# A third expert's second matrix loaded ahead, with the memory map and the load order changed to make room

## The chip, the cores and the metric

One core of a Trainium2 chip runs the whole program. The metric is the device time of one execution in microseconds (us); lower is better. The engines are TensorE (PE in the profile, its weight loads PEld), VectorE (DVE), ScalarE (ACT), GpSimd (POOL) and SyncE (SP); an engine's own queue of transfers and waits is written SPq or ACTq.

## The reference, cut to what matters

Two decoder layers over 512 tokens of width 1024, all in float32. Each layer has a mixer (layer 0: sliding-window attention and RWKV-7; layer 1: gated linear attention), a cross-attention into 256 memory tokens, and a hierarchical mixture of experts (MoE). In the MoE a token picks one group of 8 experts, then its two best experts in it. Of 32 experts each has three matrices of 2 MB:

```
y = (silu(x @ w1[e]) * (x @ w3[e])) @ w2[e]      # w1, w3: 1024 x 512, w2: 512 x 1024
x = x + sum over the token's two experts of gate * y
```

So both layers together read 64 experts of 6 MB, some 400 MB.

## The kernel before

**Places.** SBUF holds XT (the residual, transposed), HT (16 KB a partition), a ring of six 16 KB tiles W0 to W5, and a 72 KB region WORK that is laid out anew for each stage. Within WORK the cross-attention has its scaled input XC at 40 to 56 KB (what the queries are made from) and a head's turned scores xpT at 56 to 60 KB; the MoE has hk (the normalised rows) and later WX at 8 to 24 KB, routing tables from 24 KB, and the expert loop's own tiles (xg, xgT, ysb, hs, sl, act, spread) from 42 KB.

**The expert loop.** Expert blocks have 64 rows and are taken in pairs, i = 0, 1, 2, ...; both layers have 16 pairs here (`trips`). Block b = 0 of a pair uses W3, W4 (w1, w3) and W5 (w2), block b = 1 uses W0, W1 and W2. The order on PE for a pair is: `up(0, i)` (16 products of w1 and w3), `down(1, i-1)` (8 products of w2), turning the hidden rows, `up(1, i)` with the previous pair's results added to XT between its steps (`add_tiles`), turning, `down(0, i)` with the turning of the next pair's rows in its middle. At `k == 4` an `up` counts `hh_half`, at its end `hh_done`; a `down` counts `y_done`.

**Loads.** SP issues the weight loads, all in one queue. A buffer is loaded again as soon as its readers are through: `up(b, i)` on SP waits for `hh_half` and loads the first halves of w1 and w3 (two transfers of 1 MB), then waits for `hh_done` and loads the second halves; `down(b, i)` waits for `y_done` and loads w2 (one transfer of 2 MB). Buffers hold one pair, so a load is issued about a pair before its use.

**What is loaded ahead.** Block 0's expert goes into W3 to W5 long before (`first_expert`). Block 1's three matrices are issued in `experts` when the cross-attention's output product is through (`res_done`), since W0 to W2 hold that stage's weights until then. The third expert (pair 1, block 0) takes its w1 into HT after the rows have been turned (`h_turned`) and its w3 into WX, which lies over hk and so waits until hk has been read and stored to HBM (`rows_made`, `h_stored`; ACT stores the rows into `hrows`, from which POOL gathers each pair's rows by index into xg). Its w2 goes into W5 like any later one, when block 0 of pair 0 is done. The stream of the remaining loads begins when the routing tables are there (`plan_v`): SP then reads the number of trips and each expert's number from SBUF.

```
sp.wait_ge(s["res_done"], 16 * (L + 1))
up_weights(L, 1, slice(1, 2))
down_weights(L, 1, slice(1, 2))
sp.wait_ge(s["h_turned"], TT * (L + 1))
extra_matrix(HT, ...)
sp.wait_ge(s["rows_made"], 4 * L + 2)
sp.wait_ge(s["h_stored"], 16 * TT * (L + 1))
extra_matrix(WX, ...)
sp.wait_ge(s["plan_v"], PLAN_V * (L + 1))
```

**After layer 0's loop** the last `down`, four `add_tiles` on PE with an addition each on DVE, squares on ACT and their sum on POOL lead into layer 1's first projection, whose weights od_q, od_k, od_v0 are loaded into W0, W1, W2.

Of the kernel before, what the change touches and what calls it, by code (L numbers as in the profile page):

```python
# [18 lines left out]
I32 = mybir.dt.int32  # L19
# [4 lines left out]
P = 128  # L24
SEQ, D, MEM = 512, 1024, 256
# [18 lines left out]
BLK = 64  # L44
# [12 lines left out]
SUM_BANKS = ((0, 1), (5, 7))  # L57
MEMORY_AT = ((0, 1, 2), (3, 4, 5), (6, 7))
# [94 lines left out]
def trunk(nc, a, hrows, out):  # L153
    with ExitStack() as ctx:
# [160 lines left out]

        lg, lx = tab("lg", [P, TT, NR]), tab("lx", [P, TT, NX])
# [11 lines left out]
        nit, nitf = tab("nit", [P, 2], I32), tab("nitf", [P, 2])  # L328
        bei, bef = tab("bei", [P, NBLK], I32), tab("bef", [P, NBLK])
        idx = tab("idx", [P, NPAIR], I32)  # L330
        slot_gate, slot_tok = tab("slot_gate", [P, NPAIR]), tab("slot_tok", [P, NPAIR])
        rhot, comb = tab("rhot", [P, 8, HB]), tab("comb", [P, 8, 2, NBLK])
        cmp = tab("cmp", [P, (NBLK - NX) * NX])
        M3 = WORK + 42 * KB
        assert table[0] <= M3
        xg = sb("xg", [P, D], at=M3)
        xgT = sb("xgT", [P, 2, KD, BLK], at=M3 + 4 * KB)
        ysb = sb("ysb", [P, D], at=M3 + 8 * KB)
        hs = [sb(f"hs{b}", [P, FF], at=M3 + 12 * KB + 2 * KB * b) for b in range(2)]
        sl = [sb(f"sl{b}", [P, 4, BLK], at=M3 + 16 * KB + KB * b) for b in range(2)]  # L340
        act_ = [sb(f"act{b}", [P, 4, BLK], at=M3 + 18 * KB + KB * b) for b in range(2)]
        spread = sb("spread", [P, 2 * P], at=M3 + 20 * KB)
        osb = sb("osb", [P, TT, D], at=WORK + 24 * KB)
# [36 lines left out]
        def _(sp):  # L380
# [34 lines left out]

            def up_half(L, b, e, half):
# [9 lines left out]
            def down_weights(L, b, e):  # L426
                sp.dma_start(W4[EXPERT[b] + 2], a["moe_w2"][L][e][0].rearrange("(p k) n -> p k n", p=P)).then_inc(w2_in[b], 16)

            def extra_matrix(dst, matrix):
                sp.dma_start(dst[:, :, :], matrix.rearrange("(p k) n -> p k n", p=P)).then_inc(s["extra_in"], 16)  # L430

            def experts(L, pairs):
# [33 lines left out]
                down(0, 1)  # L466
                down(1, 1)
                up(1, 2)
                down(0, 2)
# [1986 lines left out]
```

## Time and profile before

| | |
|---|---|
| median of 3 runs | 1855.28 us (1853.74 to 1870.42) |
| the profiled execution | 1862.81 us, its span 1861.0 us, mean granted clock 0.99 |
| PE busy | 1754.9 us (94%) |
| DVE, ACT, POOL busy | 539.8, 524.4, 169.5 us (29%, 28%, 9%) |
| chain that ended last | PE 57%, DMA 35% of the span |
| moved by DMA | 466.40 MB; HBM read 468.12 MB |

A busy PE here is one with matmuls in flight. The times in the sections below are of this one profiled execution, in us from its start. Layer 0's expert loop lies at about 514 to 993, layer 1's at about 1370 to 1846.

### The profile page before, as it was taken

What the parts mean: (1) busy time and instruction counts of PE and PEld (TensorE: products, weight loads), DVE (VectorE), ACT (ScalarE), POOL (GpSimd) and SP (SyncE); (2) the same over time, 40 slices, a digit from 0 to 9 for tenths busy, and PEclk for the clock granted to TensorE, in tenths of its full rate; (3) what the DMA queues carried; (4) which work ended last, traced back from release to release, by engine and by line L of the source; (5) the groups of instructions that cost most, each with busy time, mean ns of one, the idle gap of its engine ahead of it and who ended that gap; (6) DMA issues with size and microseconds to landing.
All of it is one profiled execution on the core that took longest, in us unless ns stands there. A gap on an engine that the chain in (4) does not pass through costs nothing.

```text
span 1861.0 us, 23577 instructions
## 1 busy us (share of the span) xinstructions
PE 1754.9 (94%) x9202; PEld 844.7 (45%) x9202; DVE 539.8 (29%) x973; ACT 524.4 (28%) x934; POOL 169.5 (9%) x208
## 2 busy tenths in 40 slices
PE   8999899999999989898999999999999998989898
PEld 4555777455433333333334443686443333333333
DVE  2154555322332313131313004212242231313133
ACT  3244342243422221212123004423332222121213
POOL 2000351020100000000001000221100000000000
PEclk9999799999999999999999999999999999999999
DMA  7210100160399999999994113104099999999995
GB/s 193 91 46 1 47 2 2 68 255 20 130 391 422 423 422 423 424 423 421 418 390 173 47 45 133 48 1 184 0 375 424 423 423 422 423 424 423 423 421 201
DMA packets 88564, 466.40 MB, mean 251 GB/s; under 512 B 22319, under 2 KB 24479, under 8 KB 48058
## 3 DMA queue, kind: packets, MB, share of 16 engines
q1 hardware_dynamic: 77600, 450.98, 59.8%
q0 software_dynamic: 4608, 7.92, 1.2%
q10 hardware_dynamic: 6298, 6.68, 1.1%
q8 instruction: 43, 0.70, 0.2%
q14 instruction: 15, 0.12, 0.0%
HBM read 468.12 MB, written 6.29 MB: 255 GB/s over the span
## 4 chain that ended last, share of the span: by engine, by line
PE 57%; DMA 35%; DVE 4%; ACT 2%; SPq 1%; issue 1%; POOL 0%; ACTq 0%; DVEq 0%; POOLq 0%
PE ps L1092 52%; DMA W<-in_moe_w 33%; PE ps L1301 2%; DMA hrows<-hk 2%; SPq L419 1%; ACT hk L1015 0%; DVE CS L1987 0%; PE ps L1782 0%; PE ps L1819 0%; DVE XI L2120 0%; POOL sqo L600 0%; DMA xin<-in_x 0%; PE ps L1530 0%; PE ps L1238 0%; DVE XJ L2056 0%
## 5 line engine op out<-in xcount | busy, mean ns | idle before, releaser
L1092 PE MATMUL ps<-W,xgT 128*64 128x512 f32 x1984 | 458.2, 599 | 24.4 <-DMA W<-in_moe_w 22.9
L1092 PE MATMUL ps<-HT,W 128*128 128x512 f32 (+2 forms) x896 | 337.4, 533 | 4.3 <-DVE HT L1952 1.4
L1092 PE MATMUL ps<-W,act 128*64 128x512 f32 x1024 | 240.0, 601 | 33.4 <-DMA W<-in_moe_w 33.4
L1092 PEld LDWEIGHTS ps<-W,xgT 128*64 128x64 f32 x1984 | 131.2, 136 | 273.3 <-issue 235.7
L1092 PEld LDWEIGHTS ps<-HT,W 128*128 128x128 f32 (+1 forms) x896 | 166.3, 188 | 163.1 <-issue 151.0
L1048 ACT ACTIVATE ysb<-ps 32x512 f32<-32x512 f32 x248 | 146.0, 589 | 267.2 <-PE ps L1092 265.0
L2381 DVE TENSOR_TENSOR XT<-ps,XT 128x512 f32<-128x512 f32 x248 | 159.6, 685 | 182.8 <-PE ps L1092 182.8
L2375 DVE TENSOR_TENSOR act<-ps,sl 128x256 f32<-128x256 f32 x64 | 26.9, 420 | 473.8 <-ACT sl L1041 473.8
L1037 ACT ACTIVATE hs<-ps 128x512 f32<-128x512 f32 x64 | 38.2, 597 | 441.5 <-PE ps L1092 441.5
L1092 PE MATMUL ps<-spread,ysb 64*128 64x256 f32 x992 | 140.4, 402 | 3.2 <-DVE ysb L2401 1.7
L1092 PEld LDWEIGHTS ps<-W,act 128*64 128x64 f32 x1024 | 65.9, 136 | 160.4 <-issue 107.9
L1092 PEld LDWEIGHTS ps<-spread,ysb 64*128 64x128 f32 x992 | 85.6, 186 | 108.0 <-DVE XT L2381 49.6
L633 POOL COPY idc<-idx 128x1 int32 (+1 forms) x32 | 5.8, 182 | 862.7 <-PE ps L1782 804.7
L1092 PE MATMUL ps<-W,HT 128*128 128x512 f32 (+1 forms) x192 | 63.2, 488 | 0.0
L1092 PE MATMUL ps<-xo,W 128*128 128x512 f32 x128 | 56.3, 595 | 0.0
L1092 PE MATMUL ps<-XC,W 128*128 128x512 f32 x128 | 56.1, 592 | 0.0
L2371 DVE COPY xgT<-ps 128x1024 f32<-128x1024 f32 x32 | 39.2, 1224 | 51.5 <-PE ps L1782 51.5
L1933 DVE TENSOR_TENSOR XT<-ps,XT 128x512 f32<-128x512 f32 (+1 forms) x32 | 20.0, 624 | 115.1 <-PE ps L1092 115.1
L1092 PEld LDWEIGHTS ps<-W,HT 128*128 128x128 f32 x192 | 31.4, 191 | 32.2 <-issue 32.2
L1819 PEld LDWEIGHTS ps<-ident,hs 128*128 128x128 f32 x256 | 26.8, 140 | 40.6 <-issue 24.3
L1819 PE MATMUL ps<-ident,hs 128*128 128x128 f32 x256 | 42.0, 287 | 2.8 <-ACT hs L1037 2.8
L1782 PEld LDWEIGHTS ps<-ident,xg 128*128 128x128 f32 x256 | 27.4, 141 | 27.5 <-issue 24.3
(422 smaller groups left out, 1598.6 us busy)
## 6 DMA issues: line engine op xcount, KB each, us to landing
W<-in_moe_w SPq DMA_DIRECT2D x248, 1024.0 KB, 17.8
W<-in_moe_w SPq DMA_DIRECT2D x64, 2048.0 KB, 23.4
W<-in_od_w_in SPq DMA_DIRECT2D x6, 2048.0 KB, 8.1
W<-in_ev_w_in SPq DMA_DIRECT2D x3, 2048.0 KB, 7.8
W<-in_xa_wq SPq DMA_DIRECT2D x2, 2048.0 KB, 8.5
W<-in_xa_wo SPq DMA_DIRECT2D x2, 2048.0 KB, 11.9
hrows<-hk ACTq DMA_DIRECT2D x8, 512.0 KB, 15.8
HT<-in_moe_w SPq DMA_DIRECT2D x2, 2048.0 KB, 16.9
```

The lines of the kernel that those rows point to most:

```text
L419: sp.dma_start(W8[EXPERT[b]][:, k4, :], w1[:, k4, :]).then_inc((wa_in, w13_in)[half][b], 16)
L633: g.tensor_copy(idc[:, :], column).then_inc(s["gb_step"], 1)
L1037: sc.activation(hs[b][:, :].rearrange("p (k q) -> p k q", k=4), ps[:, 2 + b, :].rearrange("p (q k) -> p k q", k=4), ACT.Copy).then_inc(s[" ...
L1048: ins = sc.activation(ysb[o:o + HB, 512 * h:512 * h + 512], ps[r:r + HB, 6, :], ACT.Copy)
L1092: return te.matmul(o, l, r, start=first, stop=last)
L1301: return te.matmul(o, l, r, start=first, stop=False, skip_group_check=True)
L1782: ins = te.transpose(ps[:, k // 4, P * (k % 4):P * (k % 4) + P], xg[:, k * P:k * P + P], ident[:, :])
L1819: ins = te.transpose(ps[:, 4, f * P:f * P + P], hs[b][:, f * P:f * P + P], ident[:, :])
L1933: ve.tensor_tensor(XT[:, mt, cols], ps[:, at + mt % 2, cols], XT[:, mt, cols], ALU.add).then_inc(s["xt_ready"], 1)
L2371: ve.tensor_copy(by_rows(xgT), ps[:, 0:2, :].rearrange("p w (g b c) -> p (w g) b c", g=8, b=2)).then_inc(s["xgT_in"], 1)
L2375: ve.tensor_tensor(act_[b][:, :, :], ps[:, 4, :].rearrange("p (f c) -> p f c", f=4)[:, :, BLK:2 * BLK], sl[b][:, :, :], ALU.mult).then_inc ...
L2381: return ve.tensor_tensor(x, ps[:, SUM_BANKS[m % 2][h], :].rearrange("p (k t q) -> p k t q", k=2, t=2), x, ALU.add)
```

## The change

- Each layer loads the third expert's w2 ahead as well, into a new tile WY at 44 to 60 KB of WORK, over XC and xpT of head 2 (`extra_second`, after `sm_pv` has counted head 2's product). PE's `down(0, 1)` reads it there. The load of w2 for pair 1, block 0, into W5 is gone; W5 takes pair 2's at that place instead (`down(0, 2, readers=1)`), ahead of `down(1, 1)`.
- Block 1's matrices are issued as each ring tile comes free. Layer 0: w1 and w3 after the memory values (`DONE["xv"]`), then WY, then w2 after the output product. Layer 1: w2 after the mixer's output product, w1 after the queries, WY, and w3 (whole, `up_matrix`) after the cross-attention's output product.
- Every load of a w2 and of a third expert's matrix is made of two transfers of half the size.
- Hidden rows, gates, activations and results (hs, sl, act, ysb) lie from 26 KB of WORK, over routing tables that are no longer read; the tables still read in the loop stand below 26 KB. xg, xgT, spread and osb move.
- At the end of layer 0, od_q and od_k are loaded once the last `up` is through (`hh_done`), od_v0 as before; the four `add_tiles` write four different pairs of PSUM banks, and only the last one waits for a DVE addition, the first.

```
+FINAL_BANKS = ((5, 7), (4, 6), (2, 3), (5, 7))
...
+        OVER = WORK + 26 * KB
...
+        spread = sb("spread", [P, 2 * P], at=WORK + 42 * KB)
+        WY = sb("WY", [P, 4, D], at=WORK + 44 * KB)
+        xg = sb("xg", [P, D], at=WORK + 4 * KB)
+        xgT = sb("xgT", [P, 2, KD, BLK], at=WORK + 60 * KB)
+        hs = [sb(f"hs{b}", [P, FF], at=OVER + 2 * KB * b) for b in range(2)]
...
+            def up_matrix(L, b, e, m):
+                w = a[("moe_w1", "moe_w3")[m]][L][e][0].rearrange("(p k) n -> p k n", p=P)
+                for half, k4 in enumerate((slice(0, 4), slice(4, 8))):
+                    sp.dma_start(W8[EXPERT[b] + m][:, k4, :], w[:, k4, :]).then_inc((wa_in, w13_in)[half][b], 16)
...
             def down_weights(L, b, e):
-                sp.dma_start(W4[EXPERT[b] + 2], a["moe_w2"][L][e][0].rearrange("(p k) n -> p k n", p=P)).then_inc(w2_in[b], 16)
+                w2 = a["moe_w2"][L][e][0].rearrange("(p k) n -> p k n", p=P)
+                for f in (slice(0, 2), slice(2, 4)):
+                    sp.dma_start(W4[EXPERT[b] + 2][:, f, :], w2[:, f, :]).then_inc(w2_in[b], 16)
...
             def extra_matrix(dst, matrix):
-                sp.dma_start(dst[:, :, :], matrix.rearrange("(p k) n -> p k n", p=P)).then_inc(s["extra_in"], 16)
+                n = dst.shape[1]
+                m = matrix.rearrange("(p k) n -> p k n", p=P)
+                for part in (slice(0, n // 2), slice(n // 2, n)):
+                    sp.dma_start(dst[:, part, :], m[:, part, :]).then_inc(s["extra_in"], 16)
+
+            def extra_second(L):
+                sp.wait_ge(s["sm_pv"], 7 + 4 * L)
+                extra_matrix(WY, a["moe_w2"][L][EXTRA:EXTRA + 1][0])
...
-                def down(b, i):
+                def down(b, i, readers=0):
                     e = expert(b, i)
-                    sp.wait_ge(s["y_done"], i * 2 + (pairs * 2 + (b + L + 1)))
+                    sp.wait_ge(s["y_done"], (i - readers) * 2 + (pairs * 2 + (b + L + 1)))
+                    if readers:
+                        sp.sem_inc(w2_in[b], 32)
                     down_weights(L, b, e)
 
-                sp.wait_ge(s["res_done"], 16 * (L + 1))
-                up_weights(L, 1, slice(1, 2))
-                down_weights(L, 1, slice(1, 2))
+                if L == 0:
+                    sp.wait_ge(s["proj_done"], DONE["xv"][1])
+                    up_weights(L, 1, slice(1, 2))
+                    extra_second(L)
+                    sp.wait_ge(s["res_done"], DONE["xo0"][1])
+                    down_weights(L, 1, slice(1, 2))
+                else:
+                    sp.wait_ge(s["res_done"], DONE["od_o1"][1])
+                    down_weights(L, 1, slice(1, 2))
+                    sp.wait_ge(s["proj_done"], DONE["xq1"][1])
+                    up_matrix(L, 1, slice(1, 2), 0)
+                    extra_second(L)
+                    sp.wait_ge(s["res_done"], DONE["xo1"][1])
+                    up_matrix(L, 1, slice(1, 2), 1)
...
                 up(0, 2, readers=1)
                 up(1, 1)
-                down(0, 1)
+                down(0, 2, readers=1)
                 down(1, 1)
                 up(1, 2)
-                down(0, 2)
                 with sp.Fori(3, trips) as i:
...
-            sp.wait_ge(s["y_done"], pairs * 2 + 2)
+            sp.wait_ge(s["hh_done"], pairs * 2 + 2)
             for name, _ in LOADS[LAYER0_LOADS:]:
+                if name == "od_v0":
+                    sp.wait_ge(s["y_done"], pairs * 2 + 2)
                 load(name)
...
-                    if m >= 2:
-                        pe.wait_ge(s["xt_ready"], n["xt"] + 2 * (m - 1))
-                    add_tiles(m)
+                    if m == 3:
+                        pe.wait_ge(s["xt_ready"], n["xt"] + 2)
+                    add_tiles(m, FINAL_BANKS[m])
```

## Rows read from the trace of the kernel before

**Rows 1.** The page: the span in 40 slices of 46.5 us, busy tenths.

```profile
PE   8999899999999989898999999999999998989898
DMA  7210100160399999999994113104099999999995
```

**Rows 2.** The chain of waits that ended last: start, duration (us), work.

```profile
577.02 1.87 PE ps L1092 x8
...
605.09 1.87 PE ps L1092 x8
...
610.59 22.81 DMA W<-in_moe_w
...
695.33 4.89 PE ps L1092 x24
...
726.34 4.89 PE ps L1092 x24
...
972.73 11.80 PE ps L1092 x64
...
1493.56 23.76 DMA W<-in_moe_w
...
1825.67 11.80 PE ps L1092 x64
```

**Rows 3.** Windows: length, busy us by engine, granted clock, DMA share, GB/s.

```profile
500.00:518.00 18.00, 15.20 (x112) 9.02 (x114) 14.91 (x67) 9.34 (x13) 0.00 (x0) 1.00 1.02 427
...
532.00:552.00 20.00, 18.56 (x94) 6.75 (x92) 2.07 (x3) 5.94 (x11) 1.19 (x2) 1.00 1.02 424
552.00:560.00 8.00, 8.00 (x44) 3.08 (x46) 3.86 (x6) 0.23 (x1) 0.00 (x0) 1.00 1.02 430
...
1530.00:1800.00 270.00, 245.62 (x1250) 92.80 (x1248) 63.36 (x103) 59.25 (x107) 10.80 (x18) 1.00 1.01 423
```

**Rows 4.** The timeline of SP's queue, layer 0: issue time, issue duration, line, transfer.

```profile
495.79 0.33 SPq L419 DMA_DIRECT2D W<-in_moe_w  x1
...
505.67 0.33 SPq L430 DMA_DIRECT2D HT<-in_moe_w  x1
524.26 0.33 SPq L430 DMA_DIRECT2D WX<-in_moe_w  x1
526.26 0.37 SPq L419 DMA_DIRECT2D W<-in_moe_w  x1
...
569.75 0.33 SPq L419 DMA_DIRECT2D W<-in_moe_w  x1
```

**Rows 5.** The timeline of SP's queue, layer 1, the same load.

```profile
1424.42 0.34 SPq L419 DMA_DIRECT2D W<-in_moe_w  x1
```

**Rows 6.** The timeline of ACT: its first store of rows.

```profile
502.97 0.35 ACTq L1019 DMA_DIRECT2D hrows<-hk  x1
```

**Rows 7.** The chain of waits: the last store of rows.

```profile
507.58 16.60 DMA hrows<-hk
```

**Rows 8.** The timeline of DVE: the end of the routing tables.

```profile
520.59 0.15 DVE L2359 CAST nit<-nitf 128x1 int32<-128x1 f32 x1
```

**Rows 9.** The timeline of PE, both layers: in brackets, idle before and its releaser.

```profile
535.09 1.09 PE L1782 MATMUL ps<-ident,xg 128*128 128x128 f32 x8 [1.39 <-DMA xg<-hrows,idc]
...
1403.65 1.94 PE L1092 MATMUL ps<-W,xgT 128*64 128x512 f32 x8 [0.45 <-DMA W<-in_moe_w]
```

**Rows 10.** DMA issues of 524.2 to 524.5: KB, us from issue to landing.

```profile
WX<-in_moe_w SPq DMA_DIRECT2D x1, 2048.0 KB, 7.6
```

**Rows 11.** DMA issues of 570.1 to 570.5.

```profile
W<-in_moe_w SPq DMA_DIRECT2D x1, 1024.0 KB, 16.2
```

**Rows 12.** DMA issues of 1424.8 to 1425.

```profile
W<-in_moe_w SPq DMA_DIRECT2D x1, 1024.0 KB, 14.6
```

**Rows 13.** DMA issues of the whole span: a 1 MB load with no other beside it.

```profile
memin<-in_mem ACTq DMA_DIRECT2D x1, 1024.0 KB, 5.0
```

**Rows 14.** The timeline of POOL after layer 0's loop.

```profile
999.36 9.71 POOL L600 TENSOR_TENSOR sqo<-sqo 128x512 f32<-128x512 f32 x7 [38.81 <-ACT sqo L715]
```

More of the change, by code:

```diff
@@ L314, in tab @@
             return sb(name, shape, dt, at=table[0] - -(-size // 32) * 32)
+        nit, nitf = tab("nit", [P, 2], I32), tab("nitf", [P, 2])
+        bei, bef = tab("bei", [P, NBLK], I32), tab("bef", [P, NBLK])
+        idx = tab("idx", [P, NPAIR], I32)
+        slot_gate, slot_tok = tab("slot_gate", [P, NPAIR]), tab("slot_tok", [P, NPAIR])
+        OVER = WORK + 26 * KB
+        assert table[0] <= OVER
         lg, lx = tab("lg", [P, TT, NR]), tab("lx", [P, TT, NX])
@@ L327, in trunk @@
         blk, brk = tab("blk", [P, 8]), tab("brk", [P, 8])
[L328 to L331, printed above, removed]
         rhot, comb = tab("rhot", [P, 8, HB]), tab("comb", [P, 8, 2, NBLK])
         cmp = tab("cmp", [P, (NBLK - NX) * NX])
[L334 to L343, printed above, removed]
+        assert table[0] <= WORK + 42 * KB
+        spread = sb("spread", [P, 2 * P], at=WORK + 42 * KB)
[3 more added lines that the diff above has]
+        hs = [sb(f"hs{b}", [P, FF], at=OVER + 2 * KB * b) for b in range(2)]
+        sl = [sb(f"sl{b}", [P, 4, BLK], at=OVER + 4 * KB + KB * b) for b in range(2)]
+        act_ = [sb(f"act{b}", [P, 4, BLK], at=OVER + 6 * KB + KB * b) for b in range(2)]
+        ysb = sb("ysb", [P, D], at=OVER + 8 * KB)
+        osb = sb("osb", [P, TT, D], at=WORK + 44 * KB)
         fin = sb("fin", [P, D], at=WORK + 64 * KB)
@@ L1783, in turn_rows, with add_tiles @@
                     ins.then_inc(s["xg_turned"], 1)
-                def add_tiles(m):
+                def add_tiles(m, banks):
                     for k in (2 * m, 2 * m + 1):
@@ L1789, in add_tiles @@
                             r, o = slice(64 * h, 64 * h + 64), 256 * (k % 2)
-                            ins = mm(ps[:, SUM_BANKS[m % 2][h], o:o + 256], ysb[r, k * P:k * P + P], spread[r, :])
+                            ins = mm(ps[:, banks[h], o:o + 256], ysb[r, k * P:k * P + P], spread[r, :])
                     ins.then_inc(s["added"], 1)
@@ L1820, in turn_hidden, with down @@
                     ins.then_inc(s["hs_turned"], 1)
-                def down(b, i, bank=6, between=None):
+                def down(b, i, bank=6, between=None, extra=False):
                     k0 = i * 2 + (pairs * 2 + b)
                     pe.wait_ge(s["act_in"], k0 + 1)
-                    pe.wait_ge(w2_in[b], (i + 1) * 16 + pairs * 16)
+                    second = WY if extra else W4[EXPERT[b] + 2]
+                    if not extra:
+                        pe.wait_ge(w2_in[b], (i + 1) * 32 + pairs * 32)
                     if bank == 6:
@@ L1831, in down @@
                         for h in range(2):
-                            ins = mm(ps[64 * h:64 * h + 64, bank, :], act_[b][:, f, :], W4[EXPERT[b] + 2][:, f, 512 * h:512 * h + 512],
+                            ins = mm(ps[64 * h:64 * h + 64, bank, :], act_[b][:, f, :], second[:, f, 512 * h:512 * h + 512],
                                      f == 0, f == 3)
@@ L1861, in pair_of_blocks @@
                     turn_hidden(1, i)
-                    down(0, i, between=lambda: next_rows(i, first))
+                    down(0, i, between=lambda: next_rows(i, first), extra=extra)
                 pair_of_blocks(0, first=True)
@@ L2376, in gated, with add_tiles @@
                                      sl[b][:, :, :], ALU.mult).then_inc(s["act_in"], 1)
-                def add_tiles(m, h):
+                def add_tiles(m, h, banks):
                     x = XT[:, 2 * m:2 * m + 2, :].rearrange("p k (t q) -> p k t q", t=TT)[:, :, HALF_TILES[h], :]
-                    return ve.tensor_tensor(x, ps[:, SUM_BANKS[m % 2][h], :].rearrange("p (k t q) -> p k t q", k=2, t=2), x, ALU.add)
+                    return ve.tensor_tensor(x, ps[:, banks[h], :].rearrange("p (k t q) -> p k t q", k=2, t=2), x, ALU.add)
                 def pair_of_blocks(i, first=False):
@@ L2407, in moe @@
                     dve.wait_ge(s["added"], (trips + pairs) * 4 + (m + 1))
-                    add_tiles(m, 0)
-                    add_tiles(m, 1).then_inc(s["xt_ready"], 2)
+                    add_tiles(m, 0, FINAL_BANKS[m])
+                    add_tiles(m, 1, FINAL_BANKS[m]).then_inc(s["xt_ready"], 2)
                     for k in (2 * m + 1,):
```

6 lines of the change are left out of this document (3 added, 3 removed).

## The prediction

> **What bounds the kernel now.** I read the page's slices first. The expert loops are the two stretches in which DMA is at 9 of 10, and they fill half of the span; between them DMA stands nearly still, at 0 to 1 tenths while the cross-attention runs (slice 10, about 419 to 465) [rows 1]. PE is at 9 almost everywhere, so the page alone does not say which of the two sets the loop's time. The chain of waits does. Its entries in layer 0 are PE alone up to 607, and one pair takes 605.09 - 577.02 = 28.07 us; from 610.59 on each pair has one long DMA entry, and a pair takes 726.34 - 695.33 = 31.0 us [rows 2]. Layer 1 changes over at 1493.56 [rows 2]. So PE needs 28.07 us for a pair and DMA 31.0. A pair's loads are 12.58 MB and its gather of rows 0.52 MB; over 31.0 us that is 423 GB/s, which is what the windows show all through, at a DMA share of 1.01 [rows 3]. Each loop begins with loads that are ahead of PE, loses 2.9 us of that lead per pair, and from the fifth or sixth pair on is bound by the stream of loads. After the changeover the end of the loop is set by when the stream began, by its bytes, and by any pause in it. The last pair's `up(1, 15)` starts at 972.73 and 1825.67 [rows 2]; with PE alone it could have started at 577.02 + 13 x 28.07 = 941.9 in layer 0, so 31 us are to be had there at most.
>
> **What the change takes out of the stream.** 2 MB less after the gate in each layer is 2.10 MB / 423 GB/s = 5.0 us, twice. WY's load moves into the cross-attention, where DMA is idle [rows 1], behind `sm_pv`; nothing that is needed before stands behind that wait on SP, as xo0 and xo1 are issued ahead of it.
>
> **What becomes earlier.** At 495.79 SP issues block 1's 6.29 MB, and behind them share the engines the 2.1 MB of HT (505.67) and the 2.1 MB of stored rows (from 502.97) [rows 4, 6]. Together 10.5 MB, 24.8 us at 423 GB/s; the stretch 500 to 518 runs at 427 [rows 3], and the last store lands at 507.58 + 16.60 = 524.2 [rows 7], 3.6 us more than the bytes. WX waits for this and is issued at 524.26 [rows 4]. With the change only 2.1 MB are issued at 495.79 and are through by about 502.5; stores and HT take 502.97 + 9.9 + 3.6 = 516.5. So WX goes out 7.8 us earlier. The stream's first load then waits for the tables: they are ready at 520.59 + 0.15 = 520.7 [rows 8], and SP needs the 526.26 - 524.26 - 0.33 = 1.7 us that it took before to read trips and expert [rows 4], so it is issued at 522.4. WX's own data then runs to about 523.4 and the next starts at 524.3 (a load that meets an empty queue lands 7.6 us after issue, of which 5.0 are data [rows 10]), a pause of 0.9 us. Without any other limit the stream would be 7.8 + 5.0 - 0.9 = 11.9 us ahead.
>
> **What is late next.** Loads can only be issued when PE gives a buffer back, so a stream that is too far ahead meets PE. The load to look at is `up(0, 3)`, first half, whose gate is `hh_half` of pair 2. Before, it is issued at 569.75 and its second transfer (issued 570.17) lands 16.2 us later, at 586.4 [rows 4, 11], so the queue was some 8.5 us deep. 11.9 us earlier would be 574.5. The gate moves too, because POOL's gather waits for the same stores and PE waited 1.39 us for it at 535.09 [rows 9]; the gather needs the stores and the tables, so it goes from 524.2 to about 521, some 3 us earlier, and that wait is gone. The issue comes at 569.75 - 1.39 = 568.36, and with an empty queue the pair of transfers lands 7.7 us later (7.6 for one of 2 MB [rows 10], plus a little for the second issue): 576.1. That is later than 574.5, so PE's gate decides, with 1.6 us to spare. Layer 0's gain is 586.4 - 576.1 = 10.3 us. The ten loads behind it are issued 3.4 to 6 us apart, each before the data ahead of it is through, so no second pause arises, and the stream falls behind PE by 2.9 us a pair again.
>
> In layer 1 the same load is issued at 1424.42 and its second transfer (at 1424.85) lands 14.6 us later, 1439.4 [rows 5, 12]. PE's wait for a load at 1403.65, 0.45 us, goes [rows 9], so the gate is at 1423.97 and the landing at 1431.7. Ungated it would be 1439.4 - 11.9 = 1427.5. Layer 1's gain is 7.7 us. The end stays with the stream in both: 972.73 - 10.3 = 962.4 is still 22 us behind PE's 941.9 - 1.4, and in layer 1 1825.67 - 7.7 = 1818 is behind 1403.65 + 14 x 28.07 = 1796.6.
>
> **The split transfers.** Some 34 more transfers a layer, each 0.33 us on an SP queue that is idle most of the time [rows 4]: nothing. Whether smaller transfers cost rate: the stretch 532 to 552 carries 1 MB transfers (w1, w3) at 424, and 552 to 560 mostly 2 MB ones at 430 [rows 3]. If that were the transfers' size and not scatter, each w2 would take 0.08 us longer; with 13 stream-bound pairs, 2 a pair, 2 layers, 52 x 0.08 = 4.2 us lost. The long stretch with both is at 423 [rows 3], so I take 0.4 us and keep 4.2 as the bound.
>
> The Trainium skill speaks against this edit. Its page "DMA: Bandwidth & Descriptors", section "Anatomy of one DMA", fits 2.0 us plus the bytes' time for every transfer (on GpSimd's path), and under "Bandwidth" it lists 341 GB/s at 1 MB. By that a split w2 would cost 2.0 us more each, an estimate of over 100 us for the 52. The trace disagrees where transfers are queued: 1 MB ones run at 424 GB/s [rows 3].
>
> **The rest, with one answer.** The tiles over the tables add no wait: ACT's first hs is written after `hh_done` of the block in which PE reads the last table, and the loop's own tables stay clear. The order `down(0, 2)` before `down(1, 1)`: the second is used about 24 us after its gate, 5 us of delay fit. Layer 0's end: od_q and od_k leave earlier, and PE gets banks freely, but POOL's seven additions of squares follow each other with hardly a gap for 9.71 us from 999.36 [rows 14], and their start depends on the first DVE addition and on ACT, which do not move; 0 us, at most 0.5 gained. Loads during the cross-attention beside PE: PE holds its pace beside a full DMA in the loop, so 0.
>
> Sum: 10.3 + 7.7 - 0.4 = 17.6 us of the profiled execution's 1862.81, which is 7.5 us above the median. Nothing in the gain depends on that difference, so I take it off the median: 1855.3 - 17.6 = 1837.7, said 1838.
>
> **The rivals.**
> - The stream is not held by PE's gate. It takes that `up(0, 3)` is issued on a queue that is still full. For it: only 1.6 us separate the two in layer 0. Against: in layer 1 it is 4.2. Gain 2 x 11.9 = 23.8, time 1831.5.
> - Only the bytes count. The stores to HBM land no earlier, because they are slow by themselves and not by the queue; WX and stream start as before and 5.0 us a layer remain, 1845.4. For it: the last store needs 16.60 us for 0.5 MB. Against: before it stand 10 MB, and the rate in that stretch is 427 [rows 3].
> - The change does not do what it says: the lead is eaten elsewhere (the pause after WX grows, a gate that I took as hidden comes late, `wr`'s small loads are held up by the earlier weights). 1855, no change.
> - Slower: a split w2 is served as two lone transfers. A lone 1 MB takes 5.0 us [rows 13], a lone 2 MB 7.6 [rows 10], so a split would cost 2 x 5.0 - 7.6 = 2.4 us each if nothing overlapped. The place is the stream-bound part, 52 transfers: up to 125 us, 1963. It turns the sign from 17.6 / 52 = 0.34 us each. Against it stands the 424 GB/s of queued 1 MB transfers.
>
> **How the numbers follow.** The forecast has 0.62, ungated 0.11, bytes alone 0.14, no change 0.08, slower 0.05. From 1830 to 1847 the range holds the first three, with room for the 4.2 us on either a forecast or an ungated stream, about 0.82. What a measurement of this kernel can tell from no change is 1%, 18.6 us, so 1836.7 is the bound, right beside the forecast. A little under half of the forecast's cases (a gate that comes 0.5 us earlier in each layer, the end's 0.5) and all ungated ones lie below it: 0.28 + 0.11 = 0.39 faster. Slower by over 1% is 0.04, the rest, 0.57, within.
>
> **What the profile after would show.** WX issued at about 516 to 518 in layer 0, 7 to 8 us earlier than 524.26 relative to the first store; the stream's first load at 522.4, right behind the tables; `up(0, 3)` landing about 7.7 us after its issue (a full queue, over 10 us, would be the ungated rival); no PE wait for xg in pair 0; a DMA share of 1.0 from then on and a pair at 31.0 us; the chain's first long DMA entry three pairs later in both layers. Windows of mostly w2 loads below 415 GB/s would show the split's cost. The prediction is wrong if the stores still land 16 us after issue, if the changeover from PE to DMA does not move, or if a pair's 31.0 us changes.

## The result and the profile after

The changed kernel takes 1848.26 us (median of 20 runs, 1841.2 to 1864.26), and the kernel before, run beside it, 1860.97 us (20 runs, 1852.32 to 1881.45). The ratio is 0.9942, with a 95% interval of 0.9919 to 0.9965. The ratio is taken over the fast executions of both kernels and so is not quite that of the two medians. The change makes the kernel faster, by 0.6%, which is within 1%. The predicted 1838 was 10.3 us too low, and the measured time lies 1.3 us above the end of the range.

The page of the changed kernel, its 40 slices and the chain by engine:

```profile
span 1859.3 us, 23723 instructions
...
PE   8999899999999999898998999999999999999898
...
PEclk9999797899999999999999999999999999999999
DMA  7210100044399999999996112204379999999995
...
PE 70%; DMA 22%; DVE 4%; ACT 1%; issue 1%; SPq 0%; POOL 0%; DVEq 0%; POOLq 0%
```

Two things stand out beside [rows 1]. DMA is at 4 in slice 10 and at 3 in slice 29, in the two cross-attentions, where it stood at 0, and the chain gives DMA 22% where it gave 35%. The span, though, is only 1.7 us shorter (the execution 1861.11 us against 1862.81). The PEclk row says where to look: the clock is at 7 and 8 in slices 7 and 8. The granted clock of three stretches, first in the changed kernel and then in the kernel before:

```profile
15.00:20.00 5.00, 4.15 (x6) 1.84 (x7) 5.00 (x8) 0.00 (x0) 0.00 (x0) 0.66 1.34 222
170.00:350.00 180.00, 166.68 (x2109) 133.12 (x2108) 84.60 (x168) 53.74 (x112) 48.05 (x42) 0.82 0.05 13
300.00:340.00 40.00, 37.74 (x408) 31.04 (x404) 12.52 (x27) 5.44 (x12) 2.96 (x3) 0.54 0.01 1
```

```profile
15.00:20.00 5.00, 3.92 (x9) 1.81 (x10) 4.96 (x9) 0.00 (x0) 0.00 (x0) 1.00 1.35 215
170.00:350.00 180.00, 165.95 (x2141) 127.47 (x2140) 88.79 (x175) 60.80 (x114) 48.04 (x42) 0.91 0.06 18
300.00:340.00 40.00, 37.94 (x421) 25.72 (x422) 14.40 (x27) 9.24 (x15) 1.45 (x2) 0.91 0.01 1
```

From 170 to 350 us RWKV runs, whose instructions the change does not touch. In this one execution TensorE spent almost all of 300 to 340 at the lower of its two levels. So the spans can't be compared whole. I cut both at four events that every kernel here has: the issue of HT's load (the third expert's w1) and the start of `up(1, 15)`, in each layer.

| us | before | after | difference |
|---|---|---|---|
| start to HT's issue, layer 0 | 505.67 | 520.72 | +15.05 |
| from there to `up(1, 15)`, layer 0 | 467.06 | 458.20 | -8.86 |
| from there to HT's issue, layer 1 | 386.81 | 387.56 | +0.75 |
| from there to `up(1, 15)`, layer 1 | 466.13 | 457.56 | -8.57 |
| to the end | 35.33 | 35.26 | -0.07 |

The two loops gained 17.4 us, where 17.6 were forecast, and the part ahead of layer 0's loop, with RWKV in it, lost 15. The 0.75 between the loops is a matter of where a fall of the clock lies. In the changed kernel the granted clock is 0.83 from 1356 to 1366 us, just ahead of HT's issue at 1366.48, and 1.00 in the 10 us after; in the kernel before it is 1.00 from 1349 to 1359 and 0.83 from 1359 to 1369, just behind HT's issue at 1359.54. The fall, 1.7 us of lost clock, is thus counted in layer 1's loop before and in the part between the loops after. Both parts together went from 852.94 to 845.12 us, a gain of 7.8. The chain of waits after shows the loops, as [rows 2] did:

```profile
577.84 12.17 PE ps L1123 x56
...
605.90 12.17 PE ps L1123 x56
...
731.00 26.44 DMA W<-in_moe_w
...
978.92 11.80 PE ps L1123 x64
...
1576.54 25.96 DMA W<-in_moe_w
...
1763.09 4.89 PE ps L1123 x24
...
1794.19 4.89 PE ps L1123 x24
...
1824.04 11.80 PE ps L1123 x64
```

A pair that PE sets still takes 28.06 us (605.90 - 577.84). The first long DMA entry comes 210 us behind HT's issue instead of 105 in layer 0, so nearly four pairs later, and 210 instead of 134 in layer 1, so nearly three. A pair set by DMA takes 1794.19 - 1763.09 = 31.10 us. The windows that answer to [rows 3], with one of 6 us at `up(0, 3)`:

```profile
532.00:552.00 20.00, 18.60 (x122) 6.90 (x120) 6.47 (x16) 3.55 (x6) 2.53 (x4) 1.00 0.97 376
552.00:560.00 8.00, 8.00 (x40) 2.63 (x38) 0.00 (x0) 2.64 (x5) 0.06 (x1) 1.00 1.01 419
580.00:586.00 6.00, 6.00 (x32) 1.99 (x30) 0.00 (x0) 2.11 (x4) 0.08 (x1) 1.00 0.63 196
1530.00:1800.00 270.00, 253.27 (x1278) 95.88 (x1274) 64.97 (x105) 59.96 (x108) 10.77 (x18) 0.99 1.01 421
```

SP's queue in layer 0, and ACT's first store of rows, answering to [rows 4, 6]:

```profile
510.84 0.81 SPq L437 DMA_DIRECT2D W<-in_moe_w  x2
520.72 0.83 SPq L443 DMA_DIRECT2D HT<-in_moe_w  x2
531.42 0.80 SPq L443 DMA_DIRECT2D WX<-in_moe_w  x2
537.44 0.36 SPq L427 DMA_DIRECT2D W<-in_moe_w  x1
...
583.32 0.33 SPq L427 DMA_DIRECT2D W<-in_moe_w  x1
583.74 0.50 SPq L428 DMA_DIRECT2D W<-in_moe_w  x1
```

```profile
518.03 0.35 ACTq L1050 DMA_DIRECT2D hrows<-hk  x1
```

And the DMA issues, from issue to landing: the stores of rows, and the second transfer of `up(0, 3)`, first half, in layer 0 and layer 1 (before: 16.6 for the last store, then 16.2 and 14.6 [rows 7, 11, 12]; the median of the four stores was 15.8):

```profile
hrows<-hk ACTq DMA_DIRECT2D x4, 512.0 KB, 5.7
...
W<-in_moe_w SPq DMA_DIRECT2D x1, 1024.0 KB, 7.1
...
W<-in_moe_w SPq DMA_DIRECT2D x1, 1024.0 KB, 7.0
```

Read from SP's first issue near the gate (495.79 before [rows 4], 510.84 after), WX goes out 20.58 us later instead of 28.47, the stream's first load 26.60 instead of 30.47, and `up(0, 3)` 72.48 instead of 73.96. The last of the four stores lands 8.7 us after its issue. The data of `up(0, 3)` lands on an empty queue, and the window 580 to 586 shows the pause ahead of it: a DMA share of 0.63. From there on the share is 1.01 again.

### The profile page after: what moved, and what is told of

It is laid out like the page before. It is cut to its first block, busy times and chain, and to the rows that moved or that the text cites. A ratio compares the mean times of both kernels' runs of the same rounds, so it can differ in the third digit from the quotient of the medians.

```text
span 1859.3 us, 23723 instructions
## 1 busy us (share of the span) xinstructions
PE 1776.5 (96%) x9202; PEld 861.2 (46%) x9202; DVE 540.4 (29%) x973; ACT 524.0 (28%) x934; POOL 169.3 (9%) x208
## 4 chain that ended last, share of the span: by engine, by line
PE 70%; DMA 22%; DVE 4%; ACT 1%; issue 1%; SPq 0%; POOL 0%; DVEq 0%; POOLq 0%
PE ps L1123 64%; DMA W<-in_moe_w 22%; PE ps L1332 2%; PE ps L1850 1%; PE ps L1813 1%; DVE CS L2020 0%; PE ps L1561 0%; DMA xin<-in_x 0%; PE ps L1269 0%; DVE XI L2153 0%; DVE gcs L2256 0%; DVE KKt L2124 0%; SPq L437 0%; DVE XJ L2089 0%; DVE gsn L2287 0%
## 6 DMA issues: line engine op xcount, KB each, us to landing
W<-in_xa_wo SPq DMA_DIRECT2D x2, 2048.0 KB, 11.9
```

## The experiments

Three questions were open. Which part of the change gives the 17.4 us, and why are the parts not simply added? What does the split of the transfers cost, which I had put at 0.4 us with 4.2 as bound? And is the missing rest noise from the clock, or a cost that the change brings in elsewhere (the memory map, the loads beside the cross-attention, layer 0's end)? All kernels here compute the whole of the reference.

### The two kernels again

No edit. They show how much one kernel differs from itself.

> The kernel before, unchanged, as a control. Theory A: the changed kernel's profile lost 15 us before 511 us (the RWKV section at a granted clock of 0.50 to 0.77 between 290 and 360 us), in code that the change does not touch, so this kernel shows the same spread: times some 10 to 15 us apart between runs, the longer ones at a lower mean clock. Its stretch from the issue of block 1's loads (L0) to the start of up(1, 15) is 476.9 us again, within 0.5. Rival B: the dip belongs to the changed kernel (its memory map or its earlier loads); then this kernel's runs keep their clock within 0.003 of each other.

> The changed kernel, as a control on the same chip. Theory A: the two loops are shorter by 8.9 and 7.8 us as in its first profile, 16.7 together, whatever the clock did earlier; where its clock dips as before's does, the time is 16 to 17 us below before's on the same chip. Rival B: the ratio stays near 0.994 (11 us), because this kernel dips more often: its mean clock in the timed runs is lower than before's by 0.003 or more.

Measured: the kernel before 1865.84 us (12 runs, 1852.31 to 1880.12), ratio to itself 1.0023 (0.9982 to 1.0064). The changed kernel 1853.03 us (12 runs, 1839.31 to 1868.02), ratio 0.9932 (0.9893 to 0.9971). The loops of these two kernels repeat to 0.5 us: 466.74 and 466.36 before, 458.48 and 457.16 after. The part ahead of them, with the same instructions, does not: 495.6 us in this profile of the kernel before against 505.7 in the first, 506.4 in this one of the changed kernel against 520.7. The sign that rival B named for the changed kernel did come: its mean clock in the timed runs is 0.983, that of the 12 control runs of the kernel before 0.986. Falls inside its loops that cost no time (the last section) and the fall at its start are enough to account for it.

Nearly all of the scatter goes with the clock. In the 87 runs of the kernel before that stand beside the experiments, the mean granted clock goes from 0.973 to 0.997 and the time follows it with a correlation of -0.985: 1.5 us for each 0.001. A line through them leaves 1.5 us of scatter and gives 1868.5 us at a clock of 0.985. With it, kernels can be compared at equal clock to about 0.5 us with 12 runs each, where medians of the same runs differ by 5 us from batch to batch. Below I give the median, and for kernels with whole transfers also the time at 0.985, each from a line through that kernel's own runs.

### The split alone, put in and taken out

In the kernel before (`before_split`), and taken out of the changed kernel (`after_whole`, and in another batch `after_whole_b`):

```
-  sp.dma_start(W4[EXPERT[b] + 2], w2...).then_inc(w2_in[b], 16)
+  for f in (slice(0, 2), slice(2, 4)):
+      sp.dma_start(W4[EXPERT[b] + 2][:, f, :], w2[:, f, :]).then_inc(w2_in[b], 16)
   # and the same in extra_matrix; the waits count 32 in place of 16
```

> The kernel before with nothing changed but the split: w2 and the third expert's w1 and w3 in two transfers of 1 MB each. Theory A: 31.10 us a pair instead of 30.96, over some 12 stream-bound pairs and the stream before them in each layer, 2 to 3.5 us slower in all. Rival C: 30.96 us a pair, no change. The rival of a lone-transfer price (2.4 us each) would make it over 100 us slower.

> The changed kernel with each w2 and each third expert's matrix in one transfer of 2 MB again. Theory A (smaller transfers cost 0.14 us a pair): a stream-bound pair takes 30.96 us instead of 31.10, DMA at 423 instead of 421 GB/s, the loops' last pairs start 1.5 to 2 us earlier in each layer, 3 to 4 us in all against the changed kernel. Rival C (the rate differs by chip or run, not by transfer size): a pair takes 31.10 us here as well, no gain.

> The changed kernel with whole transfers, a second time, for the interval and as the version that should beat both. Theory A: loops 456.2 us each again, granted clock of 1.00 in all of both stream-bound parts (with halves there were two or more dips in each loop, 3.4 us of lost clock), a stream-bound pair in 30.96 us; time 15 to 21 us below before on the same chip, ratio 0.989 to 0.992. Rival (the first one was luck): loops near 458 as with halves.

Measured: `before_split` 1867.77 us (12 runs), ratio 1.0022 (0.9982 to 1.0062); its loops are 468.29 and 467.54 us, 2.6 more than before's in sum. `after_whole` 1845.03 us (6 runs), ratio 0.9899 (0.9846 to 0.9952), loops 456.15 and 456.28, 3.3 less than after's; `after_whole_b` 1845.88 us (12 runs, lowest 1835.33), ratio 0.9909 (0.9873 to 0.9944), loops 457.66 and 455.50. The timed runs alone do not part `after_whole` from the changed kernel (ratio 0.9932 beside it; the intervals overlap); the loops do. The windows of the stream-bound part say why. `after_whole`, then `before_split`:

```profile
1530.00:1800.00 270.00, 251.00 (x1282) 95.51 (x1280) 65.83 (x107) 59.96 (x108) 10.77 (x18) 1.00 1.01 423
```

```profile
1530.00:1800.00 270.00, 248.79 (x1242) 93.53 (x1242) 61.78 (x99) 59.08 (x106) 10.79 (x18) 0.98 1.01 421
```

423 GB/s with whole transfers, as in [rows 3], and 421 with halves, in the kernel before as in the changed one. A pair takes 1731.07 - 1700.09 = 30.98 us in `after_whole`:

```profile
1700.09 1.94 PE L1118 MATMUL ps<-W,xgT 128*64 128x512 f32 x8 [1.04 <-DMA W<-in_moe_w]
...
1731.07 1.94 PE L1118 MATMUL ps<-W,xgT 128*64 128x512 f32 x8 [1.05 <-DMA W<-in_moe_w]
```

and 31.10 in the changed kernel. Over the 12.5 pairs from the landing of `up(0, 3)` to `up(1, 15)` that is 1.5 us a layer, and the stretch itself is 388.1 us in the changed kernel and 386.2 in `after_whole` in layer 0, 388.2 and 386.6 in layer 1. The split costs some 3 us in all (2.6 where it was put in, 3.3 where it was taken out), 0.06 us for each of some 50 w2 loads.

Layer 0's loop in `after_whole_b` is 1.5 us longer than in `after_whole`, where the same 456.2 was expected. The first 7.5 us of the loop and the issue of `up(0, 3)`, in `after_whole` and then in `after_whole_b`:

```profile
520.60:528.00 7.40, 6.16 (x36) 3.51 (x37) 5.95 (x26) 4.50 (x8) 0.00 (x0) 1.00 1.04 357
...
583.19 0.34 SPq L427 DMA_DIRECT2D W<-in_moe_w  x1
```

```profile
497.50:505.00 7.50, 6.37 (x28) 3.42 (x30) 6.04 (x27) 3.65 (x6) 0.00 (x0) 0.77 1.02 352
...
561.78 0.33 SPq L427 DMA_DIRECT2D W<-in_moe_w  x1
```

A fall of the clock costs PE 1.7 us there, so it gives the buffer back later: `up(0, 3)` is issued 64.29 us behind HT's issue instead of 62.59, again on an empty queue (its second transfer lands after 7.1 us), and `up(1, 15)` starts 1.5 us later. `before_again` and `map_only` have the same fall at the same place and the same 64.29, but there a queue stands in front of this load, and their loops, 466.74 and 466.57, are no longer than the 467.06 of the kernel before. A delay of PE reaches the end of the loop only where the queue is empty. That is PE's gate, seen in two runs of one kernel.

### Quarters, and halves by partition

If it is the size of what one transfer reads in a row, quarters must cost more again (`after_quarters`, against the changed kernel):

```
-  for f in (slice(0, 2), slice(2, 4)):
+  for f in (slice(0, 1), slice(1, 2), slice(2, 3), slice(3, 4)):
```

If it is only the number of transfers, two that keep the run of 16 KB but take half of the partitions each must cost the same as the halves (`after_rows`, for w2 in the ring):

```
-  for f in (slice(0, 2), slice(2, 4)):
-      sp.dma_start(W4[EXPERT[b] + 2][:, f, :], w2[:, f, :])...
+  for r in (slice(0, 64), slice(64, 128)):
+      sp.dma_start(W4[EXPERT[b] + 2][r, :, :], w2[r, :, :])...
```

> The changed kernel with each w2 in four transfers of 0.5 MB, 4 KB runs in each partition, instead of two of 1 MB with 8 KB runs (whole: 16 KB runs). Theory A (smaller transfers or shorter runs cost rate in the stream): the pair goes from 30.96 (whole) and 31.10 (halves) to 31.2 or more, DMA at 419 to 420 GB/s, each loop 1 to 3 us longer than with halves. Rival (halves cost only by the clock dips they bring): a pair stays at 31.10.

> The changed kernel with each w2 in two transfers of 1 MB again, but each takes 64 partitions whole, so that the runs stay 16 KB long. It tells the number of transfers from the length of the runs: 31.10 us a pair and dips in the loops if the number counts, 30.96 us and no dips if the run length does. I expect the run length, because the packets went up from 88.6 to 98.4 thousand with the halves, 10 percent more for the same bytes. A third way: half the partitions load the engines unevenly, and it is slower than both.

Measured: `after_quarters` 1857.84 us (10 runs), ratio 0.997 (0.9933 to 1.0006), loops 461.7 and 461.8 us, 7.7 more than the changed kernel's in sum and more than the 1 to 3 us a loop that were expected. `after_rows` 2633.11 us (4 runs), ratio 1.4074 (1.3975 to 1.4173). The windows, `after_quarters` and then `after_rows`:

```profile
1530.00:1800.00 270.00, 249.96 (x1254) 94.25 (x1252) 65.16 (x105) 57.23 (x103) 10.77 (x18) 0.98 1.02 417
```

```profile
700.00:900.00 200.00, 126.89 (x470) 41.87 (x466) 23.59 (x37) 22.34 (x40) 4.79 (x8) 0.78 1.01 218
```

Whole, halves, quarters: 423, 421, 417 GB/s, with runs of 16, 8 and 4 KB of a partition in one transfer of w2 (w1 and w3 stay at 8 KB in all three). The run and the number of transfers change together in these three, and `after_rows`, which was to part them, failed as a test: it falls to 218 GB/s, half of the rate, with the DMA share still at 1.01. The share counts an engine as busy whatever the rate of its data, and only the GB/s beside it shows that something else was wrong. The Trainium skill, page "DMA: Bandwidth & Descriptors", section "The descriptor swizzle", gives for a transfer over all 128 partitions the engines 0 to 7 to partitions 0 to 63 and the engines 8 to 15 to the others. A 64-partition transfer that reaches half of the path would agree with a slow w2, but it does not explain the whole: w1, w3 and the gathered rows are two thirds of a pair's bytes and still go over all 128 partitions. If they ran at 423 GB/s and w2 at half of it, the mean would be some 320, an estimate; every 3 us from 704 to 800 shows 197 to 257. What slows the others too was not tried. So whether run length or count costs the 3 us stays open; the size of the cost does not.

### The parts of the gain

Block 1's matrices issued early, and nothing else (`before_early`, against the kernel before):

```
-  sp.wait_ge(s["res_done"], 16 * (L + 1))
-  up_weights(L, 1, ...); down_weights(L, 1, ...)
+  if L == 0:
+      sp.wait_ge(s["proj_done"], DONE["xv"][1]);  up_weights(L, 1, ...)
+      sp.wait_ge(s["res_done"], DONE["xo0"][1]);  down_weights(L, 1, ...)
+  else:
+      sp.wait_ge(s["res_done"], DONE["od_o1"][1]); down_weights(L, 1, ...)
+      sp.wait_ge(s["proj_done"], DONE["xq1"][1]);  up_matrix(L, 1, ..., 0)
+      sp.wait_ge(s["res_done"], DONE["xo1"][1]);   up_matrix(L, 1, ..., 1)
```

The third expert's w2 ahead, with the new map and the new end of layer 0, whole transfers, block 1's matrices as before (`third_only`):

```
+  extra_second(L)                  # WY, after sm_pv
   sp.wait_ge(s["res_done"], 16 * (L + 1))
   up_weights(L, 1, ...); down_weights(L, 1, ...)
...
-  down(0, 1)
+  down(0, 2, readers=1)
```

> The kernel before with block 1's three matrices issued as their buffers come free, as in the change, and nothing else: the third expert's w2 stays in the stream. Theory A (the gate of PE at up(0, 3) ends what an earlier stream can bring): WX goes out 7.8 us earlier, the stream without a gate would be 6.9 us ahead, just short of the gate. Each loop is 6.5 to 8.5 us shorter, counted from the issue of HT's load to the start of up(1, 15), 13 to 17 in all. Rival (only the bytes count): 0. At an equal mean clock the time follows the loops; theory B2 (earlier loads lower the clock elsewhere) has the mean clock of the timed runs near 0.983 instead of 0.988.

> The changed kernel with whole transfers, but block 1's matrices are issued after the output product, as before; the third expert's w2 is still loaded ahead. Theory A: 2.1 MB less in each layer's stream, 5.0 us a layer, no gate met: each loop 4.5 to 5.5 us shorter than before's 466 to 467 us, 10 in all. Together with the early loads alone (13 to 17) that is more than the 20.7 us that both bring in one kernel: the parts do not add up, because the gate cuts them. If there is no gate the parts add up.

Measured: `before_early` 1850.56 us (12 runs), ratio 0.9913 (0.9874 to 0.9952); `third_only` 1850.71 us (12 runs), ratio 0.9935 (0.9902 to 0.9968). Their loops, and where `up(0, 3)` stands in layer 0, counted from HT's issue:

| | WX issued | stream's first load | `up(0, 3)` issued | landed | `up(1, 15)`, layer 0 | layer 1 |
|---|---|---|---|---|---|---|
| before | 18.59 | 20.59 | 64.08 | 80.70 | 467.06 | 466.13 |
| `third_only` | 18.44 | 20.42 | 63.87 | 75.20 | 461.47 | 461.02 |
| `before_early` | 10.73 | 16.74 | 62.59 | 73.62 | 459.94 | 458.95 |
| `after_whole` | 10.83 | 16.68 | 62.59 | 69.92 | 456.15 | 456.28 |
| after | 10.70 | 16.72 | 62.60 | 70.12 | 458.20 | 457.56 |

The bytes alone give 5.6 and 5.1 us, where 5.0 each was the estimate. The early issue alone gives 7.1 and 7.2, where 7.8 - 0.9 = 6.9 was; the mean clock of its timed runs is 0.989, not the 0.983 of the rival B2. Alone, each leaves a queue in front of `up(0, 3)`; its second transfer lands 10.9 us after its issue in `third_only` and 10.6 in `before_early`:

```profile
W<-in_moe_w SPq DMA_DIRECT2D x1, 1024.0 KB, 10.9
```

```profile
W<-in_moe_w SPq DMA_DIRECT2D x1, 1024.0 KB, 10.6
```

Together they would give 25.0 us; with both, the queue is empty at this load, PE's gate decides, and 20.8 remain (`after_whole`). That is the gate of the prediction, and it costs 4.2 us of the sum: 1.8 in layer 0, where the prediction had 11.9 - 10.3 = 1.6, and 2.4 in layer 1, where it had 4.2. At equal clock (0.985) the timed runs say the same: before 1868.5, `third_only` 1858.2, `before_early` 1856.1, `after_whole` (18 runs) 1849.4, so gains of 10.3, 12.4 and 19.1.

### The rest of the edit

The new map alone, with the routing tables, the expert's tiles and osb at their new places (`map_only`):

```
+  nit, nitf, bei, bef, idx, slot_gate, slot_tok = ...   # now first among the tables
+  OVER = WORK + 26 * KB
-  hs = [sb(f"hs{b}", [P, FF], at=M3 + 12 * KB + 2 * KB * b) for b in range(2)]
+  hs = [sb(f"hs{b}", [P, FF], at=OVER + 2 * KB * b) for b in range(2)]
   # and likewise sl, act, ysb, xg, xgT, spread, osb
```

Layer 0's new end alone, its banks and the early od_q and od_k (`before_end`):

```
+FINAL_BANKS = ((5, 7), (4, 6), (2, 3), (5, 7))
-  sp.wait_ge(s["y_done"], pairs * 2 + 2)
+  sp.wait_ge(s["hh_done"], pairs * 2 + 2)
...
-  if m >= 2: pe.wait_ge(s["xt_ready"], n["xt"] + 2 * (m - 1))
+  if m == 3: pe.wait_ge(s["xt_ready"], n["xt"] + 2)
```

> The kernel before with only the changed memory map (tiles over the routing tables, the rest moved, no load changed). Theory A: loops and time as before, mean clock of the timed runs 0.985 to 0.989. Rival B3 (the map changes the program's beginning or its addresses so that the clock dips more often): a dip to 0.66 between 15 and 20 us as in all three profiles of the changed kernel, and a mean clock near 0.983, 5 to 7 us slower.

> The kernel before with only the end of layer 0 changed: od_q and od_k issued after the last up, four pairs of banks for the last four additions. Theory A (POOL's seven additions of squares set that end): from the start of up(1, 15) to the product with the sum of squares 36.5 us as before, within 0.2; time as before. Rival: up to 1 us shorter.

Measured: `map_only` 1865.26 us (12 runs), ratio 1.003 (1.0 to 1.0059), 1869.0 at equal clock, so +0.5. `before_end` 1862.07 us (12 runs), ratio 0.9968 (0.9927 to 1.0009), 1867.7 at equal clock, so -0.8. Both are nothing within their scatter, and the loops keep their length to 0.7 us (466.6 and 465.6; 466.6 and 465.4); in layer 1 the fall of the clock lies ahead of HT's issue in both, as in the changed kernel. The fall between 15 and 20 us that the rival B3 named is there in `map_only`, its 5 to 7 us are not. The row of POOL that was to hold the end, in `before_end` and in the changed kernel, against [rows 14]:

```profile
1011.77 9.69 POOL L603 TENSOR_TENSOR sqo<-sqo 128x512 f32<-128x512 f32 x7 [38.80 <-ACT sqo L718]
```

```profile
1005.52 9.69 POOL L631 TENSOR_TENSOR sqo<-sqo 128x512 f32<-128x512 f32 x7 [37.99 <-ACT sqo L746]
```

It starts 26.6 us behind `up(1, 15)` in all three (999.36 - 972.73, 1011.77 - 985.18, 1005.52 - 978.92), and takes the same. The product with the sum of squares follows 36.5 us behind `up(1, 15)` in the kernel before and 36.4 in the changed one, where PE waits 1.1 us for POOL. In `before_end` it is 36.9, 0.2 outside what was expected: there a fall of the clock (0.83 from 1010 to 1020 us) keeps PE busy until then. Three pairs of banks are in use, the fourth addition takes the first pair again.

### A fall of the clock at the start

The window 15 to 20 above shows a granted clock of 0.66 in the changed kernel and 1.00 before, in a stage that no part of the change touches; the first 24 matmuls take 12.23 us there instead of 10.54. It stood in all nine profiles of kernels with the new map or the early loads (0.53 in `before_early`, 0.66 in the others; the expectation below counts eight, one fewer), and in none of the four of the kernel before, `before_split` and `before_end`. A guess was that any change in the program's length does it. `before_longer` adds 47 waits that are already fulfilled when SP reaches them, at the very end:

```
-  sp.wait_ge(s["out_stored"], 16 * 2 * TT)
+  for _ in range(48):
+      sp.wait_ge(s["out_stored"], 16 * 2 * TT)
```

> The kernel before with 47 more waits on an already reached semaphore at the very end of SP's program: nothing changes while the work runs, only the program is longer. All eight profiles of kernels with the new map or the earlier loads show TensorE at half clock between 15 and 20 us, 1.7 us lost on the 24 first projection matmuls (12.2 instead of 10.5 us), and none of the four of the other kernels does. Theory (it hangs on where the start falls, which any edit of the program can shift, not on what the edits do): the dip can appear here too. Rival (the map or the loads cause it): no dip, 10.5 us. One look can show that an idle edit brings it; its absence would leave the matter open. Loops 466 to 467 us as before.

Measured: 1861.76 us in one run, beside 1866.24 of the kernel before, and in the same window:

```profile
15.00:20.00 5.00, 4.14 (x10) 2.00 (x11) 5.00 (x8) 0.00 (x0) 0.00 (x0) 1.00 1.31 215
```

The clock stays at its upper level, so 47 instructions more at the end of SP's program don't bring it, in this one run. `map_only` has it without the early loads and `before_early` without the new map, so it hangs on neither alone. What brings it is open. It costs 1.7 us.

## Why the prediction was right and wrong

**Right, step by step.** WX 7.8 us earlier: 7.9. The stream 3.9 us earlier, held by the tables and by SP's reading of them (nit written at 535.65, first load at 537.44): 3.9. `up(0, 3)` issued 1.39 us earlier and landing 7.7 us after its issue on an empty queue: 1.48 and 7.5. The stores no longer 16 us on their way: 5.7 at the median, 8.7 for the last. Layer 0's end 0, the map 0, the loads beside the cross-attention 0 within what shows. Two rivals fell by single rows: "not held by PE's gate" by the share of 0.63 in 580 to 586, "only the bytes" by WX's issue. The slower one, a split as lone transfers, needed 2.4 us for each; 0.06 was measured, and `before_split` is at 1.0022.

**The term of the split was mis-sized.** I took 0.4 us and measured 3: 2.6 by putting it into the kernel before, 3.3 by taking it out of the changed one. The rows that I had, 430 and 424 GB/s in two short windows [rows 3], pointed to a cost of this size: 2.10 MB take 4.95 us at 424 and 4.88 at 430, so 0.07 us a transfer and 3.6 us for the 52, where the prediction says 0.08 and 4.2. I set them aside as scatter because a long window with both kinds was at 423. That long window could not decide it: it held the mixture of before, not the one of after. The end that I kept as a bound was nearly the value. By the prediction's own sign a pair's 31.0 us had to stay; with halves it is 31.10, and 30.98 with whole transfers.

**Layer 1's gain was mis-sized, the other way.** Forecast 7.7, measured 8.6 with the split and 9.9 without it. Part of it is clock. In the kernel before, the planning behind HT's issue in layer 1 ran partly at the lower level, and the loop is 466.1 to 466.4 us long in two profiles; where the fall lies ahead of the issue, as in the changed kernel, it is 465.4 to 465.6 (`before_end`, `map_only`), and 464.2 in `before_longer`, where two falls lie ahead of it. The larger part is a wait that I put at nothing. I had `up(0, 3)` issued 0.45 us earlier in layer 1; it is issued 61.93 us behind HT's issue instead of 64.88, 2.95 earlier. In `map_only`, with no load changed and the fall where the changed kernel has it, the issue is at 64.33, and PE waits twice:

```profile
1382.90 1.09 PE L1784 MATMUL ps<-ident,xg 128*128 128x128 f32 x8 [2.02 <-DMA xg<-hrows,idc]
...
1397.20 1.94 PE L1094 MATMUL ps<-W,xgT 128*64 128x512 f32 x8 [0.46 <-DMA W<-in_moe_w]
```

Both waits are gone in the changed kernel, and 64.33 - 61.93 = 2.4 is about their sum. In the profile that I read, PE was 1.7 us later by the fall and did not meet the first one, so the gathered rows counted in layer 0's gate and not in layer 1's. I read the gate from one execution without looking at its clock.

**A match in part by luck.** The 17.4 us of the two loops against 17.6 hide two errors that cancel: without the split they gained 20.8, against the 18.0 of the forecast before its 0.4 was taken off, and the split took 3.3 back. The pause behind WX, 523.4 to 524.3 in the prediction, is also written 0.7 us early: from 516.5 + 7.6 and 522.4 + 2.6 it is 524.1 to 525.0, and its length of 0.9 is the same.

**The step that failed** is the last of the sum: "Nothing in the gain depends on that difference, so I take it off the median: 1855.3". The gain did not depend on it, but the base did. The median of those three runs stood on two runs at 1854 and 1855, while the 107 timed runs of the kernel before that stand beside the others in this study (the 12 of `before_again` not counted) have a median of 1863.3 us (mean 1864.8, standard error 0.8). From 1863.3 the forecast of the gain, 17.6, gives 1845.7, within the range and 2.6 us from what was measured. From the 1860.97 us of the 20 runs beside the changed kernel it gives 1843.4, within the range too. Of the 10.6 us between 1837.7 and 1848.26 the base then makes 1860.97 - 1855.28 = 5.7, and 4.9 are gain that did not come: 17.6 were forecast, and these two medians differ by 12.7. The profiled execution's own 1862.81 was the better base, and I took off its 7.5 us as if it were a disturbance. The clock in it was the key: 0.91 from 170 to 350 us, a section whose clock I never looked at because the change was elsewhere.

**What is left over.** The 32 timed runs of the changed kernel have a mean of 1851.8 (standard error 1.4), so the gain is 13.0 us with a standard error of 1.6. The first profiles give 17.4 in the loops, less 0.75 between them and 1.7 at the start, so 15.0. The 1.7 us at the start are a cost of the changed kernel that the prediction had at nothing, and the 0.75 belongs to the clock in layer 1. The remaining 2 us are within 1.3 standard errors and stay unexplained.

**The version that beats both** is, by its loops, the changed kernel with whole 2 MB transfers. Its two measurements stand at 0.9899 and 0.9909 against the kernel before, and its lowest run at 1835.33 is 4 us under the lowest of the changed kernel's 32. The means, 1848.8 of its 18 timed runs and 1851.8 of the changed kernel's, differ by 3.1 us, less than two standard errors; that it is faster rests on the loops (912.4 and 913.2 us in sum, against 915.8 and 915.6) and not on the times.

## What to carry to other kernels

Before a forecast is written against a median of few runs, read the granted clock of every section of the profile, the untouched ones too: what varies there is the noise of the measurement, and comparing at equal clock, or cutting the span at events that all versions share, finds 1 us where medians find 5. When two edits both bring a stream forward, look for the first load whose gate is not the queue but its consumer: from there the gains no longer add. And splitting a transfer that already keeps the queue full bought nothing here and had a small price for each load; it needs a reader that starts earlier because of it, and here both halves count into the same wait.

## What was not expected of the hardware

**Waits of 2.1 us, and the clock behind them.** With whole transfers PE waits 1.65 us ahead of the 16 matmuls of `down(1)` in a stream-bound pair, with halves 2.1, with quarters up to 2.4. Behind some of the longer waits the same 16 matmuls take 5.35 us instead of 3.65. After, `before_split`, `after_quarters` and `after_whole`:

```profile
850.78 3.65 PE L1123 MATMUL ps<-W,act 128*64 128x512 f32 x16 [2.11 <-DMA W<-in_moe_w]
...
881.90 5.35 PE L1123 MATMUL ps<-W,act 128*64 128x512 f32 x16 [2.12 <-DMA W<-in_moe_w]
```

```profile
904.95 3.65 PE L1097 MATMUL ps<-W,act 128*64 128x512 f32 x16 [2.12 <-DMA W<-in_moe_w]
```

```profile
916.00 5.35 PE L1123 MATMUL ps<-W,act 128*64 128x512 f32 x16 [2.41 <-DMA W<-in_moe_w]
```

```profile
879.89 3.65 PE L1118 MATMUL ps<-W,act 128*64 128x512 f32 x16 [1.64 <-DMA W<-in_moe_w]
```

The granted clock of 880 to 885 in the changed kernel is 0.81, and each of its loops shows two such falls, 3.4 us of lost clock a loop (3.4 and 1.7 in `after_again`); the stream-bound part of `after_whole` shows none. Here it costs no time, since PE waits for the next load anyway (the next pair's wait is 1.15 us instead of 2.1). But it lowers the mean clock of the kernels with halves by 0.003 to 0.004, so their times must not be set against the others' at equal mean clock; I did that only for kernels with whole transfers.

**The clock in RWKV.** With the same instructions, the part from the start to HT's issue took 495.6 to 520.8 us in the profiles. The granted clock from 300 to 340 was at 1.00 or 0.91 in the short ones and near 0.5 in the long ones; from 200 to 225 it was at 0.5 to 0.6 in most and near 1.00 in the others. It is a property of the run and not of one kernel: `before_end`, whose code is that of the kernel before up to there, has 0.51 from 300 to 340, the kernel before 0.91 and 1.00, and the changed kernel 0.54 and 0.91. What TensorE does there is many short matmuls (1280 of them with 64 columns or fewer, 0.25 us each, from 170 to 350 in the changed kernel) with waits for DVE between them. No experiment here tried to change it, although at up to 25 us it is worth more than the change of this study.
